# Changes between 512-token blocks worked through by token halves, in a chain of nine transformer blocks on one core

## The reference, cut to what matters

```
u = rmsnorm(h, g_pre) * (1 + scale) + shift      # adaLN, one scale/shift/gate for latents, one for context
y = body(u)                                       # swiglu, differential attention, grouped-query attention
h = h + weight * gate * rmsnorm(y, g_post)
```

## Time and profile before

| | us |
|---|---|
| median of 3 runs | 2533.99 |
| the profiled execution | 2535.15 |
| its span, first to last instruction | 2533.4 |
| PE busy | 2382.9 (94%) |
| DVE busy | 1459.4 (58%) |
| POOL busy | 1398.7 (55%) |
| ACT busy | 939.9 (37%) |

### The profile page before, as it was taken

The page is one execution under the profiler, slowest core; times in us unless marked ns, Lnnn a source line. Parts: engine busy times, 40 slices in busy tenths (PEclk is TensorE's granted clock), DMA queues, the critical chain, the costliest instruction groups (busy, mean ns, idle before and its releaser), DMA issues.

```text
span 2533.4 us, 34434 instructions
## 1 busy us (share of the span) xinstructions
PE 2382.9 (94%) x13900; PEld 2071.0 (82%) x13900; DVE 1459.4 (58%) x2152; ACT 939.9 (37%) x1514; POOL 1398.7 (55%) x632
## 2 busy tenths in 40 slices
PE   1999999999889999989999997989999999999998
PEld 1888887777677888877888886789989999989998
DVE  8999677655559996679963116563224202554320
ACT  4322222545443222224222225554444435544443
POOL 5544444322146453444544434258878886467985
PEclk8999999999899999998999998999999999999999
DMA  6455363111124553543542331135545564344554
GB/s 250 155 200 192 109 201 121 51 59 59 34 83 152 190 198 124 182 136 112 196 133 91 97 103 42 59 108 183 177 148 176 180 186 148 104 142 153 184 177 131
DMA packets 96878, 349.99 MB, mean 138 GB/s; under 512 B 10576, under 2 KB 10576, under 8 KB 96464
## 3 DMA queue, kind: packets, MB, share of 16 engines
q1 hardware_dynamic: 96720, 347.80, 41.7%
HBM read 346.71 MB, written 1.05 MB: 137 GB/s over the span
## 4 chain that ended last, share of the span: by engine, by line
PE 84%; DVE 8%; ACT 4%; issue 1%; POOL 0%; DVEq 0%; ACTq 0%
PE psum L1211 26%; PE psum L1215 26%; PE psum L1212 25%; PE psum L1410 1%; PE psum L1226 1%; DVE psum L877 1%; DVE h L1037 1%; DVE v L967 1%; ACT u_hi L694 1%; DVE y L1041 1%; PE psum L1378 1%; PE psum L1391 1%; PE psum L1383 1%; DVE stat L1128 1%; ACT prob L790 1%
## 5 line engine op out<-in xcount | busy, mean ns | idle before, releaser
L593 POOL TENSOR_TENSOR w_lo<-w_raw,w_hi 128x1024 fp32r<-128x1024 f32 (+1 forms) x522 | 1286.6, 2470 | 944.2 <-ACT w_hi L640 943.2
L1211 PE MATMUL psum<-u_hi,w_hi 128*128 128x256 f32 (+1 forms) x2848 | 961.4, 338 | 36.4 <-ACT u_hi L694 22.4
L1215 PE MATMUL psum<-u_lo,w_hi 128*128 128x256 f32 (+1 forms) x2848 | 941.2, 330 | 4.4 <-POOL u_lo L621 4.4
L1212 PE MATMUL psum<-u_hi,w_lo 128*128 128x256 f32 (+1 forms) x2848 | 937.1, 329 | 0.0
L640 ACT ACTIVATE w_hi<-w_raw 128x1024 fp32r<-128x1024 f32 (+1 forms) x522 | 538.0, 1033 | 644.7 <-PE psum L1215 620.3
L1211 PEld LDWEIGHTS psum<-u_hi,w_hi 128*128 128x128 f32 x2848 | 544.5, 191 | 107.4 <-issue 47.4
L1215 PEld LDWEIGHTS psum<-u_lo,w_hi 128*128 128x128 f32 x2848 | 543.6, 191 | 57.9 <-POOL u_lo L621 8.3
L1212 PEld LDWEIGHTS psum<-u_hi,w_lo 128*128 128x128 f32 x2848 | 544.7, 191 | 47.9 <-issue 3.4
L1211 PE MATMUL psum<-gu_hi,w_hi 128*128 128x512 f32 (+1 forms) x1056 | 354.8, 336 | 0.0
L1212 PE MATMUL psum<-gu_hi,w_lo 128*128 128x512 f32 (+1 forms) x1056 | 354.8, 336 | 0.0
L1215 PE MATMUL psum<-gu_lo,w_hi 128*128 128x512 f32 (+1 forms) x1056 | 354.8, 336 | 0.0
(11 more groups left out here) (138 smaller groups left out, 2189.9 us busy)
## 6 DMA issues: line engine op xcount, KB each, us to landing
w_raw<-in_ffn_in SPq DMA_DIRECT2D x264, 512.0 KB, 3.4
w_raw<-in_ffn_out SPq DMA_DIRECT2D x96, 448.0 KB, 3.3
ada_hi<-in_ada_w SPq DMA_DIRECT2D x48, 512.0 KB, 4.7
ada_lo<-in_ada_w SPq DMA_DIRECT2D x48, 512.0 KB, 5.4
w_raw<-in_ffn_out SPq DMA_DIRECT2D x48, 512.0 KB, 3.5
ada_out<-in_ada_w SPq DMA_DIRECT2D x32, 512.0 KB, 5.3
w_raw<-in_b_qkv SPq DMA_DIRECT2D x30, 512.0 KB, 3.3
w_raw<-in_da_in SPq DMA_DIRECT2D x24, 512.0 KB, 3.3
```

The lines of the kernel that those rows point to most:

```text
L593: pool.tensor_tensor(w_lo[:, slot, 0:cols], w_raw[:, slot, 0:cols], w_hi[:, slot, 0:cols].bitcast(F32), ALU.subtract).then_inc(lo_ready, 1)
L1211: mm(out, w_hi[:, slot, w], x_hi, start=start and n == 0, stop=False)
L1212: mm(out, w_lo[:, slot, w], x_hi, start=False, stop=False)
L1215: last = mm(out, w_hi[:, slot, w], x_lo, start=False, stop=stop and n == len(ks) - 1)
```

## The change

Blocks 0 to 3 ("split") now end by halves. The first output tiles are made whole; then come the latent halves of the last ones (tiles 6 and 7 of a feed-forward, 2 to 7 of the attention), then their context halves with the same weights. The sum of y of the latents, the residual, the new norm and the first tiles of the next block follow for the latents, and after that for the context. The places of the sums in PE's order, of the late pieces on DVE and ACT, and of the next block's heads on ACT are given by hand.

```diff
+def out_pieces(kind, tok):
+    if tok == LAT:
+        return [(j, LAT, {"ffn": 4 + j % 2, "b2": j % 2, "ga": (0, 1, 4, 5)[j % 4]}[kind]) for j in range(CH)]
+    first, banks = (6, (4, 5, 0, 1)) if kind == "ffn" else (2, (4, 5, 0, 1))
+    tail = [(j, half) for half in halves(FULL) for j in range(first, CH)]
+    return [(j, FULL, 4 + j % 2 if kind == "ffn" else j) for j in range(first)] \
+        + [(j, half, banks[i % 4]) for i, (j, half) in enumerate(tail)]
+    LATE = {"ffn": {"m": 0, "v2": 1}, "da": {"r1": 0, "r4": 1, "m": 2, "v0": 3, "v2": 4, "v4": 5}}
+    HEADS_AT = {"r4": 0, "r7": 1, "m": 2, "v0": 3, "v3": 4, "v7": 5}
+    PAIR_BANKS = (2, 4, 0)
...
-        rests(0, 2)
-        for b in BLOCKS:
-            for p, tok in enumerate(halves(b["tok"])):
-                for c in range(1, CH, 2):
-                    pool.wait_ge(uhi_ready, CH * (b["np"] + p) + c + 1)
-                    full = v1[:, c % 4, tok] if b["layer"] is None else ufull[:, c // 2 % 2, tok]
-                    pool.tensor_tensor(u_lo[:, c, tok], full, u_hi[:, c, tok].bitcast(F32), ALU.subtract).then_inc(u_ready[1], 1)
-            rests(b["t_body"] + (3 if b["n"] else 2), b["t_out"] + b["out_tiles"])
-            if b["n"] + 1 < len(BLOCKS):
-                t = b["t_out"] + b["out_tiles"]
-                for n in range(t, t + 3):
-                    if n == t + 2 and b["layer"] is not None:
-                        residual(b)
-                    rest(n)
+        rests(0, N_TILES)
+        def transition(b, nb):
+            t0 = nb["t_body"] if nb["n"] < len(BLOCKS) else N_TILES
+            def at(point):
+                i = late_piece(b, point)
+                if i is not None:
+                    piece_square(b, i)
+                if b["split"] and point in HEADS_AT:
+                    heads_to(t0 + HEADS_AT[point])
+            for p, tok in enumerate(halves(b["tok_out"])):
+                if b["layer"] is not None:
+                    rstd_y(b, p, tok)
+                    for c in range(CH):
+                        square(nb, p, tok, c)
+                        if p == 0:
+                            at(f"r{c}")
                 if p == 0:
-                    rstd_h(b, p, tok)
-            if b["n"] == 0:
-                sums(FIRST_SUMS, len(FIRST_PRODUCTS))
-                for t in range(AHEAD):
-                    head(t)
-            for p, tok in parts:
-                heads(b, p, tok, range(CH // 2))
-                if p + 1 < len(parts):
-                    rstd_h(b, *parts[p + 1])
-                heads(b, p, tok, range(CH // 2, CH))
+                    at("m")
+                rstd_h(nb, p, tok)
+                if nb["n"] < len(BLOCKS):
+                    for c in range(CH):
+                        u_high(nb, p, tok, c)
+                        if p == 0:
+                            at(f"v{c}")
+        def hacc(nb, p, tok, c):
+            if c == 0:
+                return
+            done = (CH - 1) * (nb["np"] + p) + c - 1
+            dve.wait_ge(hsq_ready, CH * (nb["np"] + p) + c + 1)
+            if c > 1:
+                dve.wait_ge(hacc_ready, done)
+            total = psum[:, RSTD, tok]
+            out = sq_of(c, tok) if c == CH - 1 else total
+            vec.tensor_tensor(out, sq_of(0, tok) if c == 1 else total, sq_of(c, tok), ALU.add).then_inc(hacc_ready, 1)
+        def v_part(nb, p, tok, c):
+            (_, m), = conds({**nb, "tok": tok})
+            vec.scalar_tensor_tensor(out=v1[:, c % 4, tok], in0=h[:, c, tok], scalar=norm_gain(nb, m, c),
+                                     in1=psum[:, RSTD, tok], op0=ALU.mult, op1=ALU.mult).then_inc(v1_ready, 1)
+            for a, e in ((0, 2), (2, 4)):
+                if a and split:
+                    pe.wait_ge(y_evac, before["pc"] + len(before["pieces"]) - 2)
+                for k in range(2):
+                    for t, bank, _ in tiles[a:e]:
+                        run(0, t, bank, [k])
+            if split:
+                y_sum(before, 1)
+            for k in range(2, CH):
+                for n, (t, bank, _) in enumerate(tiles):
+                    last = run(0, t, bank, [k])
+                    if k == CH - 1:
+                        done(last, ends(n, 0))
+            if len(parts) == 1:
+                return
+            for n, (t, bank, _) in enumerate(extra):
+                if split and n == 0:
+                    pe.wait_ge(y_evac, before["pc"] + len(before["pieces"]))
+                run(0, t, bank, range(CH))
+                if split and n == 0:
+                    h_sum(b, 1)
+            if split and not extra:
+                h_sum(b, 1)
+            full = [(n, t, bank) for n, (t, bank, tok) in enumerate(tiles) if tok == b["tok"]]
+            for k in range(6):
+                for n, t, bank in full:
+                    run(1, t, bank, [k])
+            for n, t, bank in full:
+                done(run(1, t, bank, range(6, CH)), ends(n, 1))
+            for t, bank, _ in extra:
+                run(1, t, bank, range(CH)).then_inc(tile_used, 1)
+            tiles = [(t0 + n, pair_bank(n // 2) + n % 2, tok) for n in range(6)]
+            if tok == FULL:
+                first_phase(b, tiles[:4], tiles[4:])
+            else:
+                first_phase(b, tiles[:4])
+            for m in range(3 if tok == FULL else 2, FCH):
+                pe.wait_ge(g_ready, FCH * b["f"] + m)
+            y_hook = {"ffn": (0, 1), "da": (0, 0)}.get(b["kind"])
+            h_hook = {"ffn": (1, 1), "da": (4, 0)}.get(b["kind"])
```

More of the change, by code:

```diff
@@ L179, in add_T @@
         u["turn"] = turns - 1
-    def whole(part):
-        it, _, k1, p = part
-        return k1 == CH and (p is None or p == len(halves(it["tok"])) - 1)
     def add_part(part):
@@ new lines, in output @@
+            late = tail_of(b, halves(FULL)[1]) if b["split"] else []
+            y_hook = {"ffn": (0, 1), "da": (0, 0)}.get(b["kind"])
+            h_hook = {"ffn": (1, 1), "da": (4, 0)}.get(b["kind"])
+            for i, (j, tok, bank) in enumerate(b["pieces"]):
+                early = b["kind"] in ("da", "ga") and i < 2
+                prev = bank_before(b, i)
+                if prev is not None:
+                    if b["layer"] is None:
+                        pe.wait_ge(h_ready, CH * b["rp"] + prev + 1)
+                    else:
+                        pe.wait_ge(y_evac, b["pc"] + prev + 1)
@@ L1303, in output @@
-            if b["layer"] is not None:
-                pe.wait_ge(yacc_ready, CH * n + CH + PAIR0)
-                for p, half in enumerate(halves(tok)):
-                    mm(psum[:, SSY[p], half], ones[:, :], sqsum[:, half], start=True, stop=True).then_inc(yss_ready, 1)
+                    ends = p == len(parts) - 1
+                    if early:
+                        last = blocks(t % RING, psum[:, bank, tok], moving(tok), [CH - 1], first=CH - 1, start=False,
+                                      ready=ready)
+                    else:
+                        last = blocks(split(t), psum[:, bank, tok], moving(tok), range(k0, k1),
+                                      start=p == 0, stop=ends, ready=None if i else ready)
@@ L1308, in mixer @@
+                    if not (b["split"] and tok == LAT):
+                        last.then_inc(tile_used, 1)
+                    elif ends:
+                        last.then_inc(lat_done, 1)
+                    if i in late:
+                        if (late.index(i), p) == y_hook:
+                            y_sum(b, 0)
+                        if (late.index(i), p) == h_hook:
+                            h_sum(BLOCKS[n + 1], 0)
         def mixer(b):
```

580 lines of the change are left out of this document (324 added, 256 removed).

## The result

The changed kernel takes 2559.23 us (median of 4), the kernel before 2536.15 beside it: ratio 1.0089, 95% interval 1.0071 to 1.0107. It is 23 us slower; the forecast was 2536, range 2512 to 2556. The profiled run took 2558.77 (span 2557.0). The page's line of busy time, which answers the earlier trace rows: TensorE (PE) works 37 us less than before in a span 24 us longer.

The account below looks back on a forecast made before the run. It took TensorE as busy for 94% of the span, the time outside its stream lying in the changes of block. Terms 9.5 - 11 - 11 + 3.5 + 2 + 9 = +2 on the median 2533.99 gave 2536 us, range 2512 to 2556.

Parts of the forecast that it names:

- Hidden edits: Bodies with adaLN work: three bank pairs and serial dots (0.17 us per tile) cost 0 (0 to 4).
- Into block 1: Change 0 to 1, into a mixer: lost after about 29 us, before 25.5, so +3.5 us.
- startup: Before block 0: start 14.3 us later, first six tiles 37.3 instead of 42.1 us; +9.5 us.
- changes 1 to 2 and 2 to 3: Changes into feed-forward blocks 2 and 3: halving loses less PE time, -11 us each.
- waits at the sums of h: Feed-forward change 2 to 3: PE waits 3.7 us at the first sum and 4.7 us at the second.
- no wait for g in front of the second pair: Feed-forward blocks with adaLN work: the second-pair stall is gone since six tiles are at hand.
- fifth tile of blocks 5 to 8: Latent blocks: the fifth tile's head stands behind the first tile's evacuation; 3 us of stall, 1.5 of half clock behind it.
- 35.9 + one w_lo + 6.7 + 1.4 = 45.0: Change 2 to 3: end of DVE's context chain, counted from the end of tile 7's latent half.
- Rival 2: Changes of block: chains shorter than laid out, w_lo beside ACT's work, about 18 us won: 2517; chance 0.24.
- Rival 4: Changes of block: overlap not had, PE waits as long in other places: 2546; chance 0.10.
- Rival 3: Changes and latent starts: short stalls amid dense work bring more half clock, slower: 2554; chance 0.24.
- the 7 us that I had named as my mark: Changes of block: the forecast is wrong if half clock covers more than 7 us of one.

Follow-up runs that it names:

- e15: Changed kernel with only the adaLN tiles of pair 1 issued ahead of weight tiles 6 and 7: 2551.8 us, ratio 1.0056.
- e2: Changed kernel with the two dots of a body's adaLN tile overlapping again: 2549.9 us, ratio 1.0055.
- e17: Changed kernel with third Silu buffer, pair 1's adaLN tiles ahead, new startup order, six heads before blocks 5 to 8, late mixer heads, overlapping dots: 2519.48 us.
- e19: e17 with the cast (gu_hi) on ACT behind the gate tile's head and gu_lo between the next pair's adaLN tiles: 2515.32 us, ratio 0.9910.
- e3: Changed kernel with the head of the tile four on placed ahead of the gu_lo wait and Silu on ACT: 2562.01 us, ratio 1.0111.
- e18: Kernel before, with both dots of each adaLN tile of the bodies serial: 2540.44 us, ratio 1.0009.
- e14: Changed kernel with a third Silu buffer and only pair 1's adaLN tiles issued ahead of weight tiles 6 and 7: 2563.82 us, ratio 1.0102.
- e12: Changed kernel in which evacuations of the first four items of blocks 1 and 4 no longer make the next two tiles' heads: 2552.34 us, ratio 1.0061.
- e7: Changed kernel with the heads of tiles 5 and 6 made ahead of the first tile's evacuation in blocks 5 to 8: 2546.98 us, ratio 1.0045.
- e6: Changed kernel with all 32 dots of the first adaLN tiles on DVE and none of their products on GpSimd: 2557.46 us, ratio 1.0088.

## Why the prediction was wrong

**The step that failed is "Hidden edits".** It put the bodies at 0 (0 to 4) because DVE "has 2 us left"; they cost 23.1 us, and the miss of 23 us is this term. The one row of DVE in a body behind those 2 us is the window of 200 to 300 us, with DVE busy for 86.78 of 100 (1.4 us a step). That window ran past the last adaLN step. In the kernel before, DVE is busy in its first part (here 150 to 260) without a rest, and hardly in its last:

```profile
150.00:260.00 110.00, 110.00 (x487) 91.09 (x487) 108.56 (x133) 26.09 (x30) 55.17 (x21) 1.00 0.56 194
280.00:300.00 20.00, 20.00 (x90) 16.57 (x89) 7.86 (x7) 4.67 (x6) 9.57 (x4) 1.00 0.34 98
```

Two edits then met there. Six tiles at once, with adaLN tiles queued behind weight tiles, make DVE late, which costs 7 us in the time (e15); the forecast did not follow what the loads of a body stand behind in the sync engine's queue. And serial dots take about 0.3 us a step that DVE did not have; taking them away gives 9 us back (e2). With both taken away, in e17, the bodies still cost 2.5 to 4 us each, since both w_lo of a step stand at their full price; e19 takes these off too. The kernel before ran without loss since one w_lo of each settled step lay partly beside the product and since DVE began blocks 2 and 3 ahead. One code can run at either pace (e3 and e18, each in one execution). What decides it in each case is not settled: e14, late by less than the changed kernel, lands in the slower one in all bodies.

**Into block 1**: the term of +3.5 measured +7.2. The gap in front of the first scores was put at 2.3 us and is 6.18; e12 shows the 3.8 of difference to be two w_lo on DVE's rotations, the contention that the prediction had priced but not placed there. The fourth item, taken forward, gives back 4.0 of its 5.4 us.

**Right in mechanism and size**: startup (first matmul 76.99 for 77.4; +8.0 for +9.5, the six tiles won 1.2 more); changes 1 to 2 and 2 to 3; waits at the sums of h of 3.2 and 4.5 us (3.7 and 4.7 forecast) and of 5.8 in the change into block 1 (7 forecast); no wait for g in front of the second pair; 2.8 to 3.0 us at the fifth tile of blocks 5 to 8 (3 forecast), shown by e7. How near the 4.7 us come is in part luck: the line "35.9 + one w_lo + 6.7 + 1.4 = 45.0" gives 46.1 with the 2.1 us of a w_lo, so 5.8 us of wait, and the 33.8 ahead of it holds with two w_lo from 21.2 on, not with the four named. The adders and gains that read PSUM did not wait for w_lo, as the earlier trace rows let expect; by form, x count | busy us, mean ns, beside u_lo, which reads SBUF alone:

```profile
L1030 DVE SCALAR_TENSOR_TENSOR u_lo<-v,mcol,u_hi 128x256 fp32r<-128x256 f32 x88 | 56.4, 641 | 4.9 <-ACT u_hi L720 4.9
...
L1020 DVE SCALAR_TENSOR_TENSOR v<-h,a_col,psum 128x256 f32<-128x256 f32 x88 | 40.8, 472 | 10.7 <-ACT psum L687 10.7
...
L1015 DVE TENSOR_TENSOR psum<-psum,sq 128x256 f32<-128x256 f32 x75 | 31.8, 425 | 2.8 <-ACT sq L703 1.0
```

**The rivals.** Rival 2 named that gain too high: the latent sums found PE waiting 3.2 us all the same. Rival 4 falls, since the two changes into feed-forward blocks won 24 us. Rival 3 is half told: half clock covers more than the 7 us that I had named as my mark (10.2 us in the change 2 to 3, 23.8 in the change 0 to 1), yet those changes came out at or near their sums. The longest stretch, behind the wait for the context sum of block 1 (length, busy us, granted clock 0.50, the lower of the two levels, 1.2 GHz):

```profile
476.40:486.60 10.20, 6.67 (x27) 5.94 (x28) 7.39 (x20) 5.45 (x12) 0.00 (x0) 0.50 0.01 2
```

Much of it lies where PE is idle or fed slowly anyway, so the mark was a bad one. Over the whole execution the mean granted clock is 0.977, before 0.975, so the clock did not get worse by the change. No rival had DVE as the bound in the bodies. The one that should have been there: a late DVE at a demand of 10.88 or more. At the 0.43 us a step measured since, 48 steps make 21 us.

## What to carry over

Read an engine's reserve from one period of its work, start to start, not from the mean of a window that may hold other work: an engine busy for 87% of a window had none while the adaLN work ran in it. Before a step is moved, follow what its loads are queued behind, and ask what a late start does to an engine that cannot catch up. Where two engines hold each other up, count the price at the worst phase; if that sum is above the pace of the bound, take work away (e19), since the good phase, as in the kernel before, may be luck.

## What was not expected of the hardware

The price of one and the same w_lo depends on which operation it meets, 1.57 to 2.2 us, and even a 128x2 operation of 0.23 us then takes 2.17. With no reserve, this gives one program two steady paces, 10.88 and 11.37 (e3) or 10.88 and 11.52 us a step (e18), and once settled at 10.88 or one of these a body kept its pace to the last adaLN step. Handing a product to GpSimd in the startup saved DVE a dot of 1.18 us and cost it 2.10 where a dot met it (six of ten products, e6).
